# Weights laid out in runs of one piece each, and new marks for the clock that spreads the expert work

## The reference

```python
h = rms_norm(x, norm_mix)
# one projection; its columns go to the three mixers
a_qkv, a_z, a_beta, a_alpha, b_f, b_i, b_q, b_g, c_qa, c_kva, c_kpe = split(h @ w_in)
o_a = gated_delta_chunked(...)     # gated delta rule, 4 heads of 128
o_b = hgrn2_chunked(...)           # HGRN2, 4 heads of 64
o_c = chunk_causal_attention(...)  # latent attention, 4 heads
x = x + concat(o_a, o_b, o_c) @ w_out
# experts (PEER), per token: 8 heads, each picks 16 of 128 * 128 experts
q = rms_norm(x, norm_ffn) @ w_query
s = q . sub_keys ; eidx, gate = the 16 best pairs of each head
act = gelu(xb . expert_u[eidx])
x = x + (gate * act) @ expert_v[eidx]
```

## Time and profile before

| | us |
|---|---|
| median of three runs | 4538.84 (4531.81 to 4553.06) |
| the profiled execution | 4519.11, span 4517.3 |
| busy in the span: PE, DVE, ACT, Pool | 2480.7, 2517.9, 923.4, 2510.7 |
| stage 0 (to the second meeting behind it) | 838.8 |
| stages 1, 2, 3 | 959.7, 1057.6, 939.2 |
| the last experts alone | 722.0 |

### The profile page before, as it was taken

How to read it: one execution, slowest core, us unless ns; L and a number is a source line. 1 busy time by engine, 2 the same in 40 slices (tenths; PEclk the granted TensorE clock), 3 DMA queues, 4 the chain that set the end, 5 groups by cost and what they waited for, 6 DMA issues and landing times. The chain is left out here.

```text
span 4517.3 us, 40216 instructions
## 1 busy us (share of the span) xinstructions
PE 2480.7 (55%) x12930; PEld 1533.1 (34%) x12930; DVE 2517.9 (56%) x6395; ACT 923.4 (20%) x2178; POOL 2510.7 (56%) x2180
## 2 busy tenths in 40 slices
PE   7656790265565782665657881365566871023355
PEld 5546570153242450543433540243242540000011
DVE  3344359785566137968666267775665148854400
ACT  2242414111312104123323113111312112000000
POOL 0000004885667456766556457876677557777765
PEclk9758795587687896876878995687687985555566
DMA  4000225798889998987778997898899998999999
GB/s 140 29 3 15 61 68 187 268 370 306 322 289 367 322 370 315 344 276 274 252 274 305 321 378 284 297 384 294 293 338 364 360 335 298 369 366 362 370 367 342
DMA packets 521060, 1273.72 MB, mean 282 GB/s; under 512 B 51130, under 2 KB 239354, under 8 KB 520724
## 3 DMA queue, kind: packets, MB, share of 16 engines
q0 software_dynamic: 313344, 1140.99, 68.8%
q1 hardware_dynamic: 190868, 114.96, 8.8%
q10 hardware_dynamic: 16640, 15.21, 1.0%
HBM read 1265.84 MB, written 4.31 MB: 281 GB/s over the span
## 5 line engine op out<-in xcount | busy, mean ns | idle before, releaser
L2420 POOL DMA_INDIRECT slots<-in_peer_expert_u,table x1088 | 1375.9, 1265 | 1309.1 <-DVE table L1909 717.4
L1926 DVE SCALAR_TENSOR_TENSOR slots<-slots,xe 128x1024 f32<-128x1024 f32 x1088 | 1294.0, 1222 | 488.8 <-DMA slots<-in_peer_expert_u,table 328.4
L2420 POOL DMA_INDIRECT slots<-in_peer_expert_v,table x1088 | 1134.6, 1043 | 682.4 <-issue 297.7
L1171 PE MATMUL ps<-slots,band 128*32 128x512 f32 x4352 | 755.7, 828 | 764.5 <-DMA slots<-in_peer_expert_v,table 666.3
L1171 PEld LDWEIGHTS ps<-slots,band 128*32 128x32 f32 x4352 | 159.9, 135 | 1203.6 <-issue 1158.3
L702 PE MATMUL ps<-region_h,region_w 128*128 128x288 f32 (+1 forms) x1024 | 290.9, 445 | 108.1 <-DMA region_w<-in_w_in 80.4
L1139 PE MATMUL ps<-region_h,region_w 128*128 128x288 f32 (+1 forms) x1024 | 264.5, 414 | 31.7 <-DMA region_w<-in_peer_w_query 29.0
L702 PEld LDWEIGHTS ps<-region_h,region_w 128*128 128x128 f32 x1024 | 217.2, 218 | 180.7 <-DMA region_w<-in_w_in 92.7
L721 PE MATMUL ps<-arena,region_h 128*128 128x256 f32 (+5 forms) x1120 | 233.2, 365 | 42.7 <-DMA arena<-in_w_in 37.5
L1139 PEld LDWEIGHTS ps<-region_h,region_w 128*128 128x128 f32 x1024 | 198.6, 199 | 114.7 <-DMA region_w<-in_peer_w_query 42.3
L721 PEld LDWEIGHTS ps<-arena,region_h 128*128 128x128 f32 (+1 forms) x1120 | 183.7, 184 | 99.6 <-DMA arena<-in_w_in 41.3
(11 more groups left out here) (369 smaller groups left out, 3629.7 us busy)
## 6 DMA issues: line engine op xcount, KB each, us to landing
region_w<-in_w_in SPq DMA_DIRECT2D x64, 512.0 KB
region_w<-in_peer_w_query SPq DMA_DIRECT2D x64, 512.0 KB
slots<-in_peer_expert_u,table POOLq DMA_INDIRECT x1088
slots<-in_peer_expert_v,table POOLq DMA_INDIRECT x1088
arena<-in_w_in ACTq DMA_DIRECT2D x12, 1024.0 KB
arena<-in_w_out SPq DMA_DIRECT2D x12, 1024.0 KB
arena<-in_w_in SPq DMA_DIRECT2D x8, 1024.0 KB
region_h<-in_w_out SPq DMA_DIRECT2D x4, 1024.0 KB, 16.1
```

What stands on the lines that cost most here:

```text
L1171: mm = nc.tensor.matmul(ps[32 * j:32 * j + 32, 6 + half_, :], window(m % BAND, row), ring[places.slot((1, m))][:, half_ * 512:(half_ + 1) ...
L1926: V.scalar_tensor_tensor(rows, rows, 1.0, xe[:, u, :], ALU.mult, ALU.mult, accum_out=own).then_inc(x_.u_free, 1)
L2420: G.indirect_dma_start(ring[slot], None, rows, bass.IndirectOffsetOnAxis(ap=numbers, axis=0)).then_inc(loaded[slot], 16)
```

## The change

Three edits, in one diff.

- The host lays `w_in`, `peer_w_query`, `w_out` and the sub keys out anew before the launch, so that each piece is contiguous and in it each partition's share too (128 columns: 4096 bytes per partition; 256 columns: 8192 bytes). The loads keep their places, buffers and semaphores; only the source pattern differs.
- Ten small parameter vectors are joined into one array of 776 floats and loaded in one DMA instead of ten, at the beginning of a layer's first stage.
- `MARKS` has new values for hgrn, gdn, mla, out and route; the end marks stay.

```diff
+IN_PIECES = [(col, P) for col in CH_COLS] + [(col, m) for col, m, _, _ in TM_CHUNKS] + [(W_BA, 8)]
+QUERY_PIECES = [(j * P, P) for j in range(16)]
+OUT_PIECES = [(k * 256, 256) for k in range(4)]
...
-MARKS = [dict(project=0, hgrn=185, gdn=315, mla=510, out=640, route=690, end=960),
-         dict(project=0, hgrn=205, gdn=310, mla=485, out=580, route=630, end=870)]
+MARKS = [dict(project=0, hgrn=155, gdn=305, mla=525, out=670, route=715, end=960),
+         dict(project=0, hgrn=175, gdn=300, mla=495, out=600, route=640, end=870)]
...
             if g == 0:
-                for dst, src, m in small_loads:
-                    sp.dma_start(dst, src[l:l + 1, :].to_broadcast([P, m])).then_inc(q.params_ready, 16)
+                sp.dma_start(params, i.params[l:l + 1, :].to_broadcast([P, 776])).then_inc(q.params_ready, 16)
...
-        def load_column(sp, ready, weights, l, j, col):
-            sp.dma_start(wcol[j % 3].rearrange("p (c n) -> p c n", c=KC),
-                         weights[l, :, col:col + P].rearrange("(c p) n -> p c n", p=P)).then_inc(ready, 16)
+        def weight_piece(weights, l, pieces, k):
+            start, m = D * sum(m for _, m in pieces[:k]), pieces[k][1]
+            return weights[l, start:start + D * m].rearrange("(p n) -> p n", p=P)
+
+        def load_column(sp, ready, weights, l, j):
+            sp.dma_start(wcol[j % 3], weight_piece(weights, l, IN_PIECES, j)).then_inc(ready, 16)
...
-            sp.dma_start(wtm[k % 2][:, 0:KC * m].rearrange("p (c n) -> p c n", c=KC),
-                         i.w_in[l, :, col:col + m].rearrange("(c p) n -> p c n", p=P)).then_inc(ready, 16)
+            sp.dma_start(wtm[k % 2][:, 0:KC * TM_CHUNKS[k][1]], weight_piece(i.w_in, l, IN_PIECES, 16 + k)).then_inc(ready, 16)
...
-            sp.dma_start(w_out_sb[k], i.w_out[l, :, k * 256:(k + 1) * 256].rearrange("(c p) n -> p c n", p=P)).then_inc(ready, 16)
+            sp.dma_start(w_out_cols[k], weight_piece(i.w_out, l, OUT_PIECES, k)).then_inc(ready, 16)
...
-                sp.dma_start(keys[:, 8 * k:8 * k + 8, :],
-                             i.peer_sub_keys[l, 4 * k:4 * k + 4].rearrange("h s n d -> n (h s) d")).then_inc(early_q, 16)
+                sp.dma_start(span(region_v, k * 1024, 1024), i.peer_sub_keys[l, k]).then_inc(early_q, 16)
...
+def in_pieces(w, pieces):
+
+    laid = [w[:, :, col:col + m].reshape(DEPTH, KC, P, m).transpose(0, 2, 1, 3).reshape(DEPTH, -1) for col, m in pieces]
+    return np.concatenate(laid, axis=1)
```

More of the change, by code:

```diff
@@ L281, in build @@
         lb_t = piece(8)
[L282 to L285, removed]
+        params = piece(776)
+        gdn_par, gdn_gain, hgrn_gain, lora_gain, knope_gain, qnope_gain, qrope_gain = (
+            params[:, a:a + n] for a, n in ((0, 8), (8, 128), (136, 64), (200, 416), (616, 64), (680, 64), (744, 32)))
         GATES = MT * GH
@@ L450, in build @@
         KEYS = [6, 2]
-        w_out_sb = [w.rearrange("p (c n) -> p c n", c=KC) for w in [span(region_h, 0, 2048)] + [span(arena, k * 2048, 2048) for k in range(3)]]
+        w_out_cols = [span(region_h, 0, 2048)] + [span(arena, k * 2048, 2048) for k in range(3)]
+        w_out_sb = [w.rearrange("p (c n) -> p c n", c=KC) for w in w_out_cols]
         mT = [span(region_c, 1024 + k * 1024, 1024) for k in range(MT)]
@@ L511, in project_loads @@
                 sp.wait_ge(q.wcol_used, j - 2)
-                load_column(sp, q.wcol_ready[j % 3], i.w_in, l, j, CH_COLS[j])
+                load_column(sp, q.wcol_ready[j % 3], i.w_in, l, j)
             sp.wait_ge(q.tail_ready, 1)
@@ L532, in first_columns @@
             for j in range(3):
-                load_column(sp, early_w, i.w_in, l, j, CH_COLS[j])
+                load_column(sp, early_w, i.w_in, l, j)
         def first_chunks(sp, l):
@@ L537, in first_chunks @@
                 load_chunk(sp, early_w, l, k)
-            sp.dma_start(wba.rearrange("p (c n) -> p c n", c=KC),
-                         i.w_in[l, :, W_BA:W_BA + 8].rearrange("(c p) n -> p c n", p=P)).then_inc(early_w, 16)
+            sp.dma_start(wba, weight_piece(i.w_in, l, IN_PIECES, 16 + len(TM_CHUNKS))).then_inc(early_w, 16)
         def hgrn_loads(sp, l, g):
@@ L598, in route_loads @@
                 sp.wait_ge(q.wcol_used, j - 2)
-                load_column(sp, q.wcol_ready[j % 3], i.peer_w_query, l, j, j * P)
+                load_column(sp, q.wcol_ready[j % 3], i.peer_w_query, l, j)
             if s + 1 < len(STAGES):
@@ L2439, with lay_out @@
     ('s_ckv', (DEPTH, 1, DEC, 128)), ('s_kpe', (DEPTH, 1, DEC, 32))]
+def in_pieces(w, pieces):
+    laid = [w[:, :, col:col + m].reshape(DEPTH, KC, P, m).transpose(0, 2, 1, 3).reshape(DEPTH, -1) for col, m in pieces]
+    return np.concatenate(laid, axis=1)
+def lay_out(inputs):
+    laid = {name: inputs[name] for name in _INS}
+    laid["w_in"] = in_pieces(inputs["w_in"], IN_PIECES)
+    laid["peer_w_query"] = in_pieces(inputs["peer_w_query"], QUERY_PIECES)
+    laid["w_out"] = in_pieces(inputs["w_out"], OUT_PIECES)
+    laid["peer_sub_keys"] = inputs["peer_sub_keys"].reshape(DEPTH, 2, 8, P, P).transpose(0, 1, 3, 2, 4).reshape(DEPTH, 2, P, 8 * P)
+    laid["params"] = np.concatenate([laid.pop(name) for name, _ in PARAMS], axis=1)
+    return laid
 def kernel(**inputs):
@@ L2447 @@
     arrays, ins, outs = {}, {}, {}
-    for name in _INS:
-        a = np.ascontiguousarray(inputs[name])
+    for name, a in lay_out(inputs).items():
+        a = np.ascontiguousarray(a)
         arrays[f"in_{name}"] = a
```

12 lines of the change are left out of this document (4 added, 8 removed).

## The result

The changed kernel takes 4517.27 us (median of 20 runs, 4500.06 to 4530.51) where the kernel before takes 4548.50 (20 runs, 4524.36 to 4582.43). The ratio is **0.9931**, 95% interval 0.9911 to 0.9950: 31 us less. Forecast were 80 us less, so the direction was right and the size was not.

A forecast was written before the change was run, and what follows sets the result against it. DMA queues, chiefly the expert gathers, bound the kernel, with room in the chains. Stages 1 and 3 at -34 each, stage 2 -9 and stage 0 -3 sum to -80 us: 4459 us on the median, range 4390 to 4520.

The forecast's parts named there:

- The packet argument: Weight columns: packets of 4096 instead of about 500 bytes raise 284 to 378 GB/s, some 20 us less DMA work a stage.
- the rival that the layout gives nothing: Weight loads: bytes, not packets, set the rate, so only -40 us remains, 4499 us; chance 0.15.
- Projection of stage 1: About 118 gathers instead of 137, and a length near 212 us instead of 246.6.
- 1.39 us of transfers per gather: DMA price read from stage 1's column stretch; a gather taken out of a full stretch gives it back until the next engine binds.
- the rival of a wash: Attention and the chains take back what projection gives: within 0.5%, about 4530 us; chance 0.13.
- I take the marginal prices because the DMA engines there have room: Gathers added to chain stretches priced from stages 2 and 0: hgrn 0.59, delta rule 0.31, attention 0.42 us each.
- the terms +8 and +4: Stages 1 and 3, 13 added gathers each: hgrn at 0.59 us is +8 us, the delta rule at 0.31 is +4.
- Stage 2's delta rule, +4 in the sum: 13 added gathers at 0.31 us each lengthen stage 2's delta rule by 4 us.
- Its hgrn, +11 in the sum: Stage 2's hgrn: 13 added dots of 1.22 us on DVE, at 0.70 of span per us, cost 11 us.
- the 1.5 that the prediction had named as its sign of being wrong: The prediction is wrong if hgrn grows by 1.5 us per added gather.
- Rival 4: hgrn and delta rule: each added dot waits 1.8 us for its row on in-order DVE; +33 us, 4572 us; chance 0.05.
- rival 2: The layout gives nothing: some 14 us in stages 1 and 3 and 12 in stage 2 go, 4499 us; chance 0.15.

The follow-up runs named there:

- chip B: Group of four jobs in which the kernel before takes about 4400 us; the changed kernel has ratios 0.9860 and 0.9846 to it there.
- chip A: Group of the first measurement and one other job, in which the kernel before takes about 4550 us; the changed kernel has ratio 0.9931 there.

## Why the prediction was wrong

**Right.** The packet argument: SP's queue fell to 6.9% (about 7% was forecast), and the rival that the layout gives nothing is refuted by 0.9836. SP's packets of 512 bytes took 29.7 ns in the mean before, 276 GB/s over sixteen engines; its packets of 4096 bytes take 174.4 ns with the layout alone, 376 GB/s, where 378 was forecast. The tail unchanged.

**Right by luck.** Projection of stage 1 came to 210.5 us (212 forecast), stage 3 alike. The price behind it, 1.39 us of transfers per gather, was not what held the stretch: with a quarter of the bytes projection took the same 236 us. The marks gave back 23 us for 17 gathers on chip B, 1.37 us each, because Pool's limit (236 us) and that of the transfers (214 us) lie close together. The time, 4517.27 us, also lies within the range by 3 us; that is its edge toward the rival of a wash, whose mechanism (the chains take back what projection gives) is what the marks alone did at 1.0025.

**The step that failed** is the sentence "I take the marginal prices because the DMA engines there have room". It has two faults. Room on the DMA engines was not what set the price in the chains: with the transfers cut to a quarter the delta rule of stage 1 still grew by 18 us for its added gathers. And the price came from a stage with another ratio of mixers to gathers. What showed in its place is a price of 1.2 to 1.9 us per added gather in stage 1's chains, of which Pool's time is one part, about half in the delta rule by the estimate above. For stages 1 and 3 the terms +8 and +4 measured +15 and +21 in stage 1, +17 and +38 in stage 3, on chip A, that of the prediction; on chip B they were +15 and +21 in stage 1. Stage 2's delta rule, +4 in the sum, was +20 on chip A and +2 in the pair on chip B. Its hgrn, +11 in the sum, was +15.7: DVE's busy time grew by 14.9 us, so a us on DVE cost 1.05 us of span and not 0.70. For 9 more gathers that is 1.7 us each, past the 1.5 that the prediction had named as its sign of being wrong. Summed over the three stages of the first profiles, hgrn and delta rule cost 127 us where 39 were counted: 88 us, more than the 49 that the timed runs fell short by, and most of the 73 that the two profiled executions did, 7 us less where 80 were forecast. Rival 4 had named a price of 1.8 us per added gather, with "such a price needs a DMA share near 1" against it. In the delta rule of stage 1 the price was 1.9 us, at a DMA share of 0.83, and the reason against it was the same mistake.

The rows to doubt it were there, though not to price it. In projection Pool is busy 184 us, and 137 gathers with 0.3 us between them make 226 of 246.6. In stage 1's delta rule it is 123 + 31 = 154 of 184: no more room than the 31 us that the DMA share of 0.83 leaves, but not less either, and enough for the 11 gathers. So counting Pool's room alone would have shown the limit in projection, and not the 21 us in the delta rule. The page's engine share of Pool, 56%, hides the first, as the time between two gathers is not counted as busy.

**The layout was undersized on chip B.** Its terms, 40 us by rival 2, were 70 there (0.9836 of 4400). That a late column also delays the slots behind it would explain this; it was argued from waits.

What made the sum small in the end, on chip B: the layout gave more than was forecast, and the marks gave less than nothing. On chip A the two were not timed apart.

**The rule of the Trainium skill that was weighed**, 512 bytes as the smallest transfer at line rate ("DMA: Bandwidth & Descriptors", Specifications), does not hold for this kernel's columns: 24.0 us for 6.82 MB in packets of 512 bytes, 276 GB/s against 376 by the packets, and the layout alone at 0.9836. A rule that was not weighed would have pointed toward Pool: the Trainium skill's page "SBUF — State Buffer", section "SBUF: two separate sides", says that DVE and GpSimd share a pair of SBUF ports under an exclusive lock, which a DVE operation takes in a two-port mode, or with two SBUF inputs against a GpSimd operation that reads SBUF, and that a DMA issued from Pool can so wait for its descriptors behind DVE. The trace agrees with the effect, 0.95 us against 1.50 with a dot beside it, and 965 against 1276 ns when the dots are short. That this dot beside a gather is such a case, and that the lock is the mechanism, no run here shows.

**Open.** Why the change gives 1.4% on chip B and 0.7% on chip A. On chip A the tail runs at 358 GB/s. On chip B the same instructions read:

```profile
3659.60:4316.30 656.70, 193.66 (x1026) 40.63 (x1026) 302.02 (x495) 16.11 (x68) 487.98 (x487) 0.66 1.00 393
```

That is 393 GB/s, and 64 us less for the same 487 gathers, so transfers run faster there. Chip A's delta rule in stage 2 grew by 20 us where chip B's grew by 2 in one pair; slower transfers alone do not explain it at a DMA share of 0.79, with Pool waiting 56.9 us for slots. The layout alone was never timed on chip A, and so its share and the marks' are not separated there beyond stages 1 and 3. What an added gather costs besides Pool's time, PE's sums above all, was not tested.

## What to carry to other kernels

Before work is moved into a stretch "with room", list for each engine and queue that the work needs what is left there, with the time between instructions counted: with the short gathers Pool was full in projection at a busy share of 80%. Room on two of them is still no proof that the work is cheap: stage 1's delta rule had 31 us on the DMA engines and 30 on Pool, and 11 gathers cost 21. A marginal price holds for the stretch from which it was read; a stage with the same line numbers but other tile counts has another. And the layout of weights paid more than its own transfers, 70 us for 40, where sums that free buffers stand behind the weights' matmuls in PE's order; that this order is the reason is likely and not shown.

## What the runs showed of the hardware that was not expected

- One indirect gather of 128 rows holds Pool for 0.94 us at the least and 0.3 us pass to the next, whether the rows are 4096 or 1024 bytes. With a quarter of the bytes the delta rule took 171.0 us against 173.0.
- A packet of 1024 bytes of a short gather took 218 ns in the mean on its DMA engine, more than one of 4096 bytes in the kernel with the layout alone (174 ns).
- With the same instructions, the tail of the two short-gather kernels took 720.8 and 653.1 us on one chip. Pool was busy 559.8 us in the longer one:

```profile
3550.20:4271.00 720.80, 198.06 (x1026) 40.96 (x1026) 301.00 (x495) 16.11 (x68) 559.81 (x487) 0.61 0.31 92
```

  Which phase the dots have against Pool's gathers may decide this; it was not tried.
- The kernel before took 4400 us in one group of jobs and 4550 in the other: 150 us, where the change brought 31 in the second.
